# A hybrid attention and mixture-of-experts block: the first expert's rows formed by fp32 products in SBUF in place of a gather from HBM

## What is computed

```
h = rms_norm(x, norm2_g)
logits = h @ w_router + b_router
top_vals, top_idx = top_k(logits, 4);  gates = softmax(top_vals)
for each expert e, for the rows xb of h that chose it, in blocks of 128:
    gu = xb @ w_gate_up[e] + b_gate_up[e]
    act = (clip(up) + 1) * (min(gate, 7) * sigmoid(1.702 * gate))
    y = act @ w_down[e] + b_down[e]
x = x + sum over a token's experts of gate * y
```

## Time and profile before

| | |
|---|---|
| median of three executions | 1665.35 us (1664.73 to 1665.51) |
| profiled execution | 1664.38 us, of it span 1662.6 us |
| TensorE busy | 1624.7 us, 98% of the span |
| VectorE, ScalarE, GpSimd busy | 1350.2, 1096.2, 311.9 us |
| first product of expert 0 | 510.27 us |
| mean DMA rate | 291 GB/s |

### The profile page before, as it was taken

The page is one execution under the profiler, slowest core; times in us unless marked ns, Lnnn a source line. Parts: engine busy times, 40 slices in busy tenths (PEclk is TensorE's granted clock), DMA queues, the critical chain, the costliest instruction groups (busy, mean ns, idle before and its releaser), DMA issues.

```text
span 1662.6 us, 24749 instructions
## 1 busy us (share of the span) xinstructions
PE 1624.7 (98%) x8080; PEld 1343.4 (81%) x8080; DVE 1350.2 (81%) x1098; ACT 1096.2 (66%) x1001; POOL 311.9 (19%) x204
## 2 busy tenths in 40 slices
PE   9999999999988999999999999999999999999995
PEld 6797877788886888888888888888888888888884
DVE  6974555423658899999999999999999999999994
ACT  5433444322455787877887777878778878778873
POOL 0000000402006523411211112211113111122110
PEclk8999999999998999999999999999999999999998
DMA  8331222432549799999999999999999999999993
GB/s 247 108 102 51 76 76 76 130 101 86 173 174 358 290 374 385 387 384 372 365 388 386 388 379 372 370 386 384 380 375 369 379 386 387 390 371 366 387 385 87
DMA packets 115018, 483.42 MB, mean 291 GB/s; under 512 B 13371, under 2 KB 56599, under 8 KB 65687
## 3 DMA queue, kind: packets, MB, share of 16 engines
q1 hardware_dynamic: 103892, 454.43, 69.9%
q0 software_dynamic: 11088, 28.48, 8.0%
HBM read 469.51 MB, written 22.26 MB: 296 GB/s over the span
## 4 chain that ended last, share of the span: by engine, by line
PE 94%; DVE 3%; ACT 1%; issue 1%; DMA 0%; POOL 0%; SPq 0%; ACTq 0%; POOLq 0%; DVEq 0%
PE ps L618 29%; PE ps L620 29%; PE ps L619 29%; PE ps L846 2%; PE ps L840 2%; DVE work L1398 2%; PE ps L727 1%; PE ps L747 1%; PE ps L876 1%; PE ps L736 1%; PE ps L882 0%; DMA r<-in_x 0%; DVE r L1406 0%; PE ps L851 0%; ACT zT L973 0%
## 5 line engine op out<-in xcount | busy, mean ns | idle before, releaser
L1274 DVE TENSOR_TENSOR zT<-raw,zT 128x2048 fp32r<-128x2048 f32 x96 | 217.7, 2294 | 47.7 <-ACT zT L973 47.7
L1274 DVE TENSOR_TENSOR zT<-more_raw,zT 128x2048 fp32r<-128x2048 f32 x96 | 220.2, 2294 | 13.4 <-ACT zT L973 13.3
L1274 DVE TENSOR_TENSOR w_lo<-raw,w_hi 128x2048 fp32r<-128x2048 f32 x96 | 219.2, 2286 | 4.6 <-ACT w_hi L973 1.3
L973 ACT ACTIVATE w_hi<-raw 128x2048 fp32r<-128x2048 f32 x96 | 184.2, 1919 | 54.6 <-PE ps L620 54.6
L1274 DVE TENSOR_TENSOR w_lo<-more_raw,w_hi 128x2048 fp32r<-128x2048 f32 x96 | 217.7, 2294 | 2.5 <-ACT w_hi L973 1.4
L618 PE MATMUL ps<-w_hi,xT 128*128 128x512 f32 x512 | 200.1, 391 | 4.6 <-DVE work L1542 3.7
L618 PE MATMUL ps<-zT,xT 128*128 128x512 f32 x512 | 202.8, 396 | 0.0
L973 ACT ACTIVATE zT<-more_raw 128x2048 fp32r<-128x2048 f32 x96 | 183.4, 1911 | 26.9 <-PE ps L620 26.9
L619 PE MATMUL ps<-w_lo,xT 128*128 128x512 f32 x512 | 199.9, 390 | 0.0
L620 PE MATMUL ps<-w_hi,xT 128*128 128x512 f32 x512 | 199.9, 390 | 0.0
L620 PE MATMUL ps<-zT,xT 128*128 128x512 f32 x512 | 199.6, 390 | 0.0
(11 more groups left out here) (261 smaller groups left out, 3295.4 us busy)
## 6 DMA issues: line engine op xcount, KB each, us to landing
more_raw<-in_w_gate_up SPq DMA_DIRECT2D x129, 1024.0 KB, 7.6
raw<-in_w_gate_up SPq DMA_DIRECT2D x127, 1024.0 KB, 8.4
raw<-in_w_down SPq DMA_DIRECT2D x65, 1024.0 KB, 8.3
more_raw<-in_w_down SPq DMA_DIRECT2D x63, 1024.0 KB, 7.6
raw<-in_w_in SPq DMA_DIRECT2D x29, 1024.0 KB, 5.4
r<-in_x SPq DMA_DIRECT2D x8, 512.0 KB, 6.2
raw<-in_w_branch_conv SPq DMA_DIRECT2D x4, 1024.0 KB, 5.3
raw<-in_w_out SPq DMA_DIRECT2D x4, 1024.0 KB, 4.9
```

Of the source, the lines that this page charges most:

```text
L973: nc.scalar.activation(expert_pair(0, c), chunk, ACT.Copy).then_inc(split_hi, 2)
L1274: nc.vector.tensor_tensor(expert_pair(1, c), chunk, expert_pair(0, c).bitcast(F32), ALU.subtract).then_inc(split_lo, 2)
```

## The change

Expert 0's rows are no longer gathered. `find(0)` writes its marks in fp32 (`first_hot`), and `select_rows(half)` multiplies them by h2 where it stands in SBUF: the stationary operand is 128 features of block b of h2 (every eighth number of a row), the moving one is the marks of block b, and four products sum over the blocks. The result in PSUM is what turned rows would be: features down, slots across. 16 products make one half, 32 both. The gather of expert 0, its `uix` column, its eight transposes and the 14 idle products are gone. Experts 1 and 2 still get their lists by `early_rows`, between the two halves. All three `find` stand in a row on VectorE, and `gather(3)` now comes first on GpSimd, ahead of the residual rows. Counters that nothing increments any more are raised by hand.

```
+        first_hot = work[:, 3584:4096].rearrange("p (b n) -> p b n", b=NB)
...
+            def select_rows(half):
+
+                for k in range(4):
+                    for b in range(NB):
+                        last = pe.matmul(ps[:, bk_T + half, P * k:P * k + P], h2[:, b, 4 * half + k::KD],
+                                         first_hot[:, b, :], start=(b == 0), stop=(b == NB - 1))
+                last.then_inc(turned_pe, 1)
+
+            pe.sem_inc(turned_pe, 1)
+            pe.wait_ge(hot_ok, 1)
+            pe.wait_ge(h2_d, 2)
+            pe.wait_ge(h2_a, 2)
+            select_rows(0)
             for e in range(1, EARLY):
                 last = early_rows(e)
             last.then_inc(early_pe, 1)
+            select_rows(1)
...
-            pe.wait_ge(early_ok, 1)
-            for _ in range(BUSY):
-                pe.matmul(ps[:, bk_D, :], oT[:, 0, 0, 0:P], oT[:, 0, 1, :], start=True, stop=True)
-            pe.wait_ge(xs_in, 16)
-            turn_rows(0)
-            turn_rows(1)
...
-            find(0)
+            for e in range(EARLY):
+                find(e)
...
-            ve.wait_ge(turned_pe, 1)
-            ve.wait_ge(ix_set, 1)
-            nc.vector.tensor_copy(stat[:, 26:27], ps[:, bk_T, 0:1]).then_inc(early_hi, 1)
-            ve.wait_ge(early_hi, 1)
-            nc.vector.scalar_tensor_tensor(uix[:, 0:1], stat[:, 26:27], float(OUT_OF_RANGE), ps[:, bk_T, 1:2],
-                                           ALU.add, ALU.add).then_inc(turned_read, 1)
...
-            gp.wait_ge(turned_read, 1)
-            gather()
+            gp.wait_ge(early_ok, 1)
+            gp.wait_ge(turned_pe, FIRST_ROWS)
+            gather(3)
```

More of the change, by code:

```diff
@@ L66 @@
 EARLY = 3
-BUSY = 14
 FIRST_BUSY = 12
@@ L821, in early_rows @@
                 for b in range(NB):
-                    last = pe.matmul(ps[:, bk_T, 2 * e:2 * e + 2], hot[:, e, b, :], tok_h[:, b, :],
+                    last = pe.matmul(ps[:, bk_D, 2 * e:2 * e + 2], hot[:, e, b, :], tok_h[:, b, :],
                                      start=(b == 0), stop=(b == NB - 1))
                 return last
-            early_rows(0).then_inc(turned_pe, 1)
-            pe.wait_ge(turned_read, 1)
+            def select_rows(half):
[9 more added lines that the diff above has]
+            select_rows(0)
             for e in range(1, EARLY):
@@ L896, in next_rows @@
                 if half == 0:
-                    pe.wait_ge(xs_in, 16 * g + 32)
+                    pe.wait_ge(xs_in, 16 * g + 16)
                     pe.wait_ge(turned_read, FIRST_ROWS if isinstance(g, int) and g == 0 else tile(g, ACT1))
@@ L1492, in find @@
             def find(e):
-                nc.vector.tensor_tensor(hot[:, e], cst[:, C_IOTA:C_IOTA + P].unsqueeze(1).to_broadcast([P, NB, P]),
+                nc.vector.tensor_tensor(hot[:, e] if e else first_hot, cst[:, C_IOTA:C_IOTA + P].unsqueeze(1).to_broadcast([P, NB, P]),
                                         sg1[:, :, e:e + 1].to_broadcast([P, NB, P]),
                                         ALU.is_equal).then_inc(hot_ok, 1)
-            find(0)
+            for e in range(EARLY):
+                find(e)
             ve.wait_ge(ranks_pe, 2)
@@ L1501, in _ @@
             link(nc.vector.tensor_scalar(nbk[:, 1:2], ps[0:NE, 2, 0:1], 2 * P + 0.5, None, ALU.is_gt))
-            ve.wait_ge(turned_pe, 1)
-            ve.wait_ge(ix_set, 1)
-            nc.vector.tensor_copy(stat[:, 26:27], ps[:, bk_T, 0:1]).then_inc(early_hi, 1)
-            ve.wait_ge(early_hi, 1)
-            nc.vector.scalar_tensor_tensor(uix[:, 0:1], stat[:, 26:27], float(OUT_OF_RANGE), ps[:, bk_T, 1:2],
-                                           ALU.add, ALU.add).then_inc(turned_read, 1)
-            for e in range(1, EARLY):
-                find(e)
+            ve.sem_inc(turned_read, 1)
             link(nc.vector.tensor_scalar(nbk[:, 2:3], ps[0:NE, 2, 0:1], 3 * P + 0.5, None, ALU.is_gt))
@@ L1513, in _ @@
             ve.wait_ge(early_pe, 1)
-            nc.vector.tensor_copy(stat[:, 27:29], ps[:, bk_T, 2:2 * EARLY:2]).then_inc(early_hi, 1)
-            ve.wait_ge(early_hi, 2)
+            ve.wait_ge(ix_set, 1)
+            nc.vector.tensor_copy(stat[:, 27:29], ps[:, bk_D, 2:2 * EARLY:2]).then_inc(early_hi, 1)
+            ve.wait_ge(early_hi, 1)
             nc.vector.scalar_tensor_tensor(uix[:, 3:5], stat[:, 27:29], float(OUT_OF_RANGE),
-                                           ps[:, bk_T, 3:2 * EARLY:2], ALU.add, ALU.add).then_inc(early_ok, 1)
+                                           ps[:, bk_D, 3:2 * EARLY:2], ALU.add, ALU.add).then_inc(early_ok, 1)
             link(nc.vector.tensor_tensor(byexp, ohk, sg1.unsqueeze(2).to_broadcast([P, NB, TOPK, NE]), ALU.mult))
@@ L1654, in _ @@
             gp.dma_start(out[S:S + P, :], x2[:, 0, :]).then_inc(out_set, 16)
-            gp.wait_ge(turned_pe, FIRST_ROWS)
-            gp.wait_ge(early_ok, 1)
-            gather(3)
             def place_records():
```

## The result

The changed kernel takes **1676.26 us** (median of four, 1676.19 to 1677.96) against 1665.43 us: a ratio of 1.0068, with a 95% interval of 1.0056 to 1.008. It is 10.8 us slower. The forecast was 1669.7 us with a range up to 1673.2: the direction was right, the size was not, and the time lies outside the range. Run again beside the last experiment, the changed kernel took 1676.12 us against 1665.35.

The account below looks back on a forecast made before the run. TensorE was taken to bound the kernel, with 94% of the last chain. Expert 0's start 2.65 us later plus 1.7 us for the clock's fall made 4.35, added to the median 1665.35: 1669.7 us, range 1667.0 to 1673.2.

Parts of the forecast that it names:

- TensorE bounds the end and a later start passes through undiminished: Whole kernel: TensorE carries 94% of the last chain, so moving expert 0's start from 510.27 moves the end equally.
- The 32 row products, 9.0 us: Ahead of expert 0 on TensorE: 9.5 products at 0.43 us, half clock, then 22.5 at 0.22, full clock.
- a spacing above 0.12 us at full clock: Sign in the row products' records that would show the forecast wrong and strided weight loads costing extra.
- Rival B: Row products: strided weight loads do not hide, 3.3 to 4.9 us more, time 1673.0 to 1674.6; chance 0.15.
- The clock's return: During the row products: TensorE's clock, at half when they begin, returns to full after 4.1 us.
- The offsets and VectorE's chunk 2 in series: Between row products and expert 0: late offsets (0.75 us) make VectorE's chunk 2 (2.28 us) delay the start to 512.9.
- The idle stretch lets the clock fall: TensorE ahead of expert 0: 3.4 us idle, 509.46 to 512.9, drops the clock to half, costing 1.7 us more.
- Rival A: Ahead of expert 0: the clock holds through the idle stretch, only 2.65 us later, time 1668.0; chance 0.34.
- Even free products would gain little: Ahead of expert 0: the order of VectorE's list sets the start, leaving hardly any room for a faster time.
- rival C: Row products cheap, 5.5 us for all 32; VectorE's list then rules, start unchanged, time 1665.4; chance 0.04.
- Mostly the transfer: Kernel before, 499.41 to expert 0's start: the 10.86 us were said to be mostly the gather's transfer.
- The time of 4.35 us in all: Total slowdown forecast: expert 0 starting 2.65 us later plus 1.7 us for the fallen clock.

Follow-up runs that it names:

- the last experiment: Changed kernel with packed operand, new list order, both idle fills and expert 2's gather issued after the ninth slot record: 1661.99 us, ratio 0.9976.
- e1: Changed kernel with the row products' stationary operand reading 128 numbers of h2 in a row, weight rows loaded to fit: 1669.96 us, ratio 1.0029.
- p1: Kernel before plus seven groups of six unused products, stationary numbers 1, 2, 4 or 8 apart; spacing per plain record 0.112, 0.118, 0.233, 0.231 us.
- e2: Changed kernel, still strided, offset products between the row-product halves, VectorE's chunk 1 ahead of the lists and first low half ahead of chunk 2: 1670.40 us.
- e4: Changed kernel with the 14 idle products put back behind the offset products: 1674.01 us, ratio 1.0052.
- e9: The changed kernel itself, unaltered, run again on the same chip and day as the other runs: 1676.12 us against 1665.35.

## Why the prediction was wrong

- **TensorE bounds the end and a later start passes through undiminished: right.** The shift is 12.0 us behind the second stretch and 11.9 at the end.
- **The 32 row products, 9.0 us: wrong, and this is the step that failed.** They took 15.5 us (499.81 to 515.59 less some 0.3 for the lists), 6.5 more. The working took the spacing of a record, 0.11 us at full and 0.215 at half clock, from the *moving* stream, and from transposes for the fact that a strided load hides. e1 shows that the numbers were right for packed rows (0.114 us); p1 shows that loads 16 and 32 bytes apart take 0.23 us, save a transpose's. The transposes were the nearest row in shape and in stride, but not in what the load does: theirs grew by 51 ns and stayed under the stream, a plain load grew by 145 and did not. The sign that the prediction named for this, a spacing above 0.12 us at full clock, is there.
- **Rival B named the cause but was priced too low and too unlikely (0.15).** Its upper bound doubled only the products at full clock, 9.0 + 4.9 = 13.9 us, on the assumption that at half clock the moving stream is the longer anyway. The spacing is 0.24 us at either clock, so all 32 pay: 15.5. The 1.6 us between the two are what 1676.3 lies above B's 1674.6. The clock's return at 506.1, 6.3 us after the first product and not 4.1, changed nothing for the same reason.
- **The offsets and VectorE's chunk 2 in series: right, to 0.1 us.** From the first offset product (515.59) to expert 0's start the trace has 4.2 us; the working had 3.45 + 0.75 = 4.2. e2 confirms the cause by taking it away.
- **The idle stretch lets the clock fall: the size right, the mechanism not borne out.** There were 3.36 us of idle against the 3.4 forecast, and expert 0 began with 3.4 us at half clock, which cost 1.6 us in the profile and 2.1 in e4's difference, against 1.7. But the clock fell at 516.36, 0.07 us before TensorE went idle, and in e9 0.65 us after; in e1, with packed products ahead of the same 3.36 us, it was still at full when expert 0 started. So the term was met partly by luck. Idle time may have kept the clock down until expert 0 came; what brought it down is open. Rival A (the clock holds) is out for this kernel all the same.
- **"Even free products would gain little" (rival C): not tested.** No run has products that cheap with the order as changed. With the order mended and the clock kept up, the products end early enough to come in 0.2% below the kernel before.
- **"Mostly the transfer": wrong, without harm to the sum.** The gather had landed by 506.5; the idle products held the turn until 508.26.
- **The time of 4.35 us in all** was thus one term short: 2.65 + 6.5 + 1.7 = 10.85 against 10.8 measured. That the two agree so closely is also luck, since the profiled executions differ by 11.9 and the 1.7 did not come about as argued.

## What to carry to other kernels

Before a transfer is replaced by products, look at how the stationary operand lies: here loads of numbers 4 and 8 bytes apart hid under 128 columns, loads 16 and 32 bytes apart did not, and reading the weight rows in another order made the operand packed at no cost that the time shows. Taking a transfer and its filling out of a chain also takes away the cover of everything that ran beside them, so the lists of the other engines have to be put in order again with the same change. Where idle products kept the clock up, see what the clock does without them: around every unfilled stretch of 3.36 or 3.66 us here it was at half, at the latest 1.4 us after the stretch. But idle products also take time: in the kernel before, the gathered rows waited for them.

## What the runs showed of the hardware

- Plain fp32 records with a load of 128 columns are 0.23 to 0.24 us apart when the load's numbers lie 16 or 32 bytes apart, and 0.11 to 0.12 at 4 and 8 bytes; reduced fp32 gives 0.238 at 32 and 0.117 at 4. At 32 bytes the plain spacing is the same at 0.50 and 1.00 of the clock. With 512 moving columns the strided load still costs 0.04 us a record (0.273 against 0.23).
- A transpose's load at the same 32 bytes costs nothing visible (0.11 us a record).
- In e2 the clock fell to half at 510.2 in the middle of strided products, with TensorE busy in every window. In the changed kernel it fell at 516.36, 0.07 us before TensorE's idle stretch, and in its second profile 0.65 us into it. The cause was not tested.
- Behind packed products the clock held through 3.36 us of idle and fell 1.1 us after the restart (e1).
